# Routed experts in five widths, each visit's TensorE work in a branch of its own, rows beyond 256 in plain fp32

## The reference, cut to what matters

```python
logits = xf @ w_router + b_router                 # 2048 x 32
top_logit, top_e = lax.top_k(logits, TOP_K)       # 4 experts of 32 for each token
gates = jax.nn.softmax(top_logit, axis=-1)
# rows of x sorted by expert, group_sizes[e] rows for expert e
hu = lax.ragged_dot(xs, w_gate_up, group_sizes) + b_gate_up[e_sorted]   # 1024 -> 2048
gate = jnp.minimum(hu[:, :D_FF], 7.0)
up = jnp.clip(hu[:, D_FF:], -7.0, 7.0)
act = (up + 1.0) * gate * jax.nn.sigmoid(1.702 * gate)
y = lax.ragged_dot(act, w_down, group_sizes) + b_down[e_sorted]         # 1024 -> 1024
out = jnp.zeros_like(xf).at[tok].add(y * g_sorted[:, None])
```

## Time and profile before

| what | value |
|---|---|
| median of 3 runs | 5028.44 us |
| the profiled execution | 5037.48 us, span 5035.6 us |
| TensorE matmul busy | 4555.1 us, 90% of the span |
| VectorE / ScalarE / GpSimd busy | 3091.1 / 1819.6 / 877.7 us |
| mean granted TensorE clock | 0.942 of full speed |
| instruction fetch queue q8 | 69 packets, 1.13 MB |
| expert stage | from about 2135 to about 4885 us |

### The profile page before, as it was taken

One profiled execution on the slowest core, in us unless ns is written; L12 is line 12 of the kernel. 1 busy time (PEld: TensorE's weight loads), 2 busy tenths in 40 slices (PEclk: granted clock), 3 DMA queues, 4 the chain that ended last, 5 costly groups with the idle time before them and its releaser, 6 DMA issues. The chain is left out here.

```text
span 5035.6 us, 67493 instructions
## 1 busy us (share of the span) xinstructions
PE 4555.1 (90%) x23694; PEld 3404.2 (68%) x23695; DVE 3091.1 (61%) x4881; ACT 1819.6 (36%) x2636; POOL 877.7 (17%) x871
## 2 busy tenths in 40 slices
PE   8999877888888886479999999999999999999987
PEld 4444333334434443378999999999899999999971
DVE  3567545766667886356465655566576556665557
ACT  1222223333333332144343444344354434454330
POOL 0000012111111111222111211112122112121125
PEclk9999977898899888789999999999999999999996
DMA  5443111000000000165554554455556455664458
GB/s 177 136 121 117 53 58 28 14 18 23 14 16 14 17 19 9 25 225 176 183 175 165 210 198 160 158 200 175 180 197 217 167 180 186 215 217 175 142 187 345
DMA packets 524040, 666.04 MB, mean 132 GB/s; under 512 B 58176, under 2 KB 388416, under 8 KB 523872
## 3 DMA queue, kind: packets, MB, share of 16 engines
q1 hardware_dynamic: 400368, 484.87, 28.8%
q10 hardware_dynamic: 96960, 93.93, 5.7%
q0 software_dynamic: 26576, 85.56, 4.4%
HBM read 543.93 MB, written 120.36 MB: 132 GB/s over the span
## 5 line engine op out<-in xcount | busy, mean ns | idle before, releaser
L1766 PE MATMUL gu<-x_hi,w_hi 128*128 128x256 f32 (+2 forms) x4096 | 1230.9, 301 | 1.3 <-DVE x_lo L1848 1.3
L1767 PE MATMUL gu<-x_lo,w_hi 128*128 128x256 f32 (+2 forms) x4096 | 1231.2, 301 | 0.0
L1768 PE MATMUL gu<-x_hi,w_lo 128*128 128x256 f32 (+2 forms) x4096 | 1229.1, 300 | 0.0
L1843 DVE TENSOR_TENSOR w_lo<-w_raw,w_hi 128x2048 fp32r<-128x2048 f32 x386 | 874.6, 2287 | 530.4 <-ACT w_hi L1917 530.4
L1917 ACT ACTIVATE w_hi<-w_raw 128x2048 fp32r<-128x2048 f32 x386 | 726.8, 1907 | 280.0 <-PE gu L1768 198.7
L1766 PEld LDWEIGHTS gu<-x_hi,w_hi 128*128 128x128 f32 x4096 | 772.2, 189 | 2.5 <-issue 1.7
L1768 PEld LDWEIGHTS gu<-x_hi,w_lo 128*128 128x128 f32 x4096 | 772.7, 189 | 0.0
L1767 PEld LDWEIGHTS gu<-x_lo,w_hi 128*128 128x128 f32 x4096 | 770.4, 188 | 0.7
L1739 POOL TENSOR_TENSOR a_lo<-up,a_hi 128x384 fp32r<-128x384 f32 x256 | 396.8, 1550 | 1489.0 <-ACT a_hi L1929 1489.0
L1766 PE MATMUL yp<-w_hi,a_hi 128*128 128x512 f32 x1296 | 525.5, 405 | 0.0
L1767 PE MATMUL yp<-w_lo,a_hi 128*128 128x512 f32 x1296 | 514.5, 397 | 0.0
(11 more groups left out here) (283 smaller groups left out, 5409.4 us busy)
## 6 DMA issues: line engine op xcount, KB each, us to landing
w_raw<-w_gate_up SPq DMA_DIRECT2D x258, 1024.0 KB, 7.1
w_raw<-w_down SPq DMA_DIRECT2D x128, 1024.0 KB, 6.2
y_dram<-y_rows ACTq DMA_DIRECT2D x192, 256.0 KB, 2.7
y_dram<-zeros ACTq DMA_DIRECT2D x12, 2688.0 KB, 14.8
h_blk<-h_dram SPq DMA_DIRECT2D x32, 512.0 KB, 6.7
qi_dram<-qi_stage ACTq DMA_DIRECT2D x16, 640.0 KB, 3.2
x_in<-x SPq DMA_DIRECT2D x16, 512.0 KB, 6.6
w_in_sb<-w_in SPq DMA_DIRECT2D x4, 2048.0 KB, 14.1
```

What stands on the lines that cost most here:

```text
L1766: nc.tensor.matmul(out, s_hi_, m_hi, start=(n == 0), stop=False)
L1767: nc.tensor.matmul(out, s_hi_, m_lo, start=False, stop=False)
L1768: op = nc.tensor.matmul(out, s_lo_, m_hi, start=False, stop=(n == len(pairs) - 1))
L1843: nc.vector.tensor_tensor(w_lo[:, c % 2, cols], raw[:, c % 3, cols], w_hi[:, c % 2, cols].bitcast(F32), ALU.subtract).then_inc(s_lo, 1)
```

## The change

Five widths (256, 288, 320, 352, 384) take the place of three. The table gets two more comparisons for `kind` and a fourth column that says whether the visit has at most 320 rows. TensorE's whole visit (up part, transposes, down part) is put inside the branch of its width, so the text of a visit stands five times in the loop. For visits with 257 to 320 rows the two tiles at places 2 and 5 go: place 2 becomes `down_rest`, 16 plain fp32 matmuls of 64 weight columns (the rows beyond 256) by 512 moving columns of the raw down weights, one half of the outputs in partitions 0 to 63 and the other in 64 to 127; place 5 becomes the tiny matmul. The raw down weights must then stay until place 2 is done, which SP waits for. POOL copies the 64 columns for it, and ScalarE stores places 2 and 5 as two halves each, whose place in memory is chosen by the new column.

```diff
-WIDTHS = (2 * P, 2 * P + 64, ROWS)
+WIDTHS = (2 * P, 2 * P + 32, 2 * P + 64, 2 * P + 96, ROWS)
+REST = 64
...
                     if not first(v) or c >= 3:
                         sp.wait_ge(s_lo, 12 * v + 2 * (c - 3) + 2)
+                    if not first(v) and c in (1, 2):
+                        sp.wait_ge(s_g2, 6 * v - 3)
...
                         pool.wait_ge(s_ah, 8 * v + j + 1)
-                        nc.gpsimd.tensor_tensor(a_lo[:, j], up[:, j % 2], a_hi[:, j].bitcast(F32), ALU.subtract
-                                                ).then_inc(s_al, 1)
+                        nc.gpsimd.tensor_tensor(a_lo[:, j], up[:, j % 2], a_hi[:, j].bitcast(F32), ALU.subtract)
+                        nc.gpsimd.tensor_copy(a_rest[:, j], up[:, j % 2, 2 * P:2 * P + REST]).then_inc(s_al, 1)
...
+                def down_rest(v):
+                    pe.wait_ge(s_lo, 12 * v + 12)
+                    for k in range(KD):
+                        for h in range(2):
+                            w = raw[:, (4 + h) % 3].rearrange("p (k n) -> p k n", k=KD)
+                            op = nc.tensor.matmul(yp[h * REST:(h + 1) * REST, 0], a_rest[:, k], w[:, k],
+                                                  start=(k == 0), stop=(k == KD - 1))
+                    return op
...
-                    for n, width in enumerate(WIDTHS):
-                        with pe.If(kind == n):
-                            up(v, width)
+                def visit(v, width):
+                    up(v, width)
                     transpose_x(v + 1, 0)
                     transpose_x(v + 1, 1)
...
-                            if m < 2:
-                                down_tile(v, c, m).then_inc(s_g2, 1)
+                            if m < 2 or width > 2 * P + REST:
+                                op = down_tile(v, c, m)
+                            elif n == 2 and width > 2 * P:
+                                op = down_rest(v)
                             else:
-                                with pe.If(kind != 0):
-                                    down_tile(v, c, m).then_inc(s_g2, 1)
-                                with pe.Else():
-                                    nc.tensor.matmul(yp[:, n % 2, 0:EXPERTS], S["ident"][:], S["so_far"][:],
-                                                     start=True, stop=True).then_inc(s_g2, 1)
+                                op = nothing(n)
+                            op.then_inc(s_g2, 1)
...
+                def body(v):
+                    kind = look_up(pe, v, 2, len(WIDTHS) - 1)
+                    pe.wait_ge(s_xl, 8 * v + 8)
+                    for n, width in enumerate(WIDTHS):
+                        with pe.If(kind == n):
+                            visit(v, width)
...
                 def body(v):
+                    rest = look_up(act, v, 3, 1)
...
-                    nc.scalar.dma_start(
-                        D_["y"][bass.ds(v * ROWS + (n % 3) * P, P), (n // 3) * BANK:(n // 3 + 1) * BANK], y[:, slot]
-                    ).then_inc(s_yst[slot], 16)
+                    if n == 2:
+                        store_half(v, n, 0, 4, 0)
+                        store_half(v, n, 1, 5 - rest, rest)
+                    elif n == 5:
+                        store_half(v, n, 0, rest + 4, 1 - rest)
+                        store_half(v, n, 1, 5, 1)
+                    else:
+                        nc.scalar.dma_start(
+                            D_["y"][bass.ds(v * ROWS + (n % 3) * P, P), (n // 3) * BANK:(n // 3 + 1) * BANK], y[:, slot]
+                        ).then_inc(s_yst[slot], 16)
```

More of the change, by code:

```diff
@@ L1606, in _ @@
                 nc.vector.tensor_scalar(start[:], left[:], float(WIDTHS[0]), None, ALU.is_gt)
-                nc.vector.tensor_scalar(nth[:], left[:], float(WIDTHS[1]), None, ALU.is_gt)
+                nc.vector.tensor_scalar(S["meta"][:, :, 3], left[:], float(2 * P + REST), None, ALU.is_le)
                 dve.drain()
-                nc.vector.tensor_tensor(S["meta"][:, :, 2], start[:], nth[:], ALU.add)
+                for width in WIDTHS[1:-2]:
+                    nc.vector.scalar_tensor_tensor(start[:], left[:], float(width), start[:], ALU.is_gt, ALU.add)
+                    dve.drain()
+                nc.vector.scalar_tensor_tensor(S["meta"][:, :, 2], left[:], float(WIDTHS[-2]), start[:],
+                                               ALU.is_gt, ALU.add)
 def experts_stage(nc, A, S, D_):
@@ L1640, in experts_stage @@
         a_lo = sb("a_lo", [P, FF // P, ROWS], F32R)
+        a_rest = sb("a_rest", [P, FF // P, REST])
         y = sb("y_rows", [P, 2, BANK])
@@ L1802, in down_tile, with nothing @@
                                                  for k in range(KD)], 8 * v if n == 0 else None)
-                def body(v):
-                    kind = look_up(pe, v, 2, 2)
-                    pe.wait_ge(s_xl, 8 * v + 8)
-                    for n, width in enumerate(WIDTHS):
-                        with pe.If(kind == n):
-                            up(v, width)
+                def down_rest(v):
[6 more added lines that the diff above has]
+                    return op
+                def nothing(n):
+                    return nc.tensor.matmul(yp[:, n % 2, 0:EXPERTS], S["ident"][:], S["so_far"][:],
+                                            start=True, stop=True)
+                def visit(v, width):
+                    up(v, width)
                     transpose_x(v + 1, 0)
@@ L1929, in high_act, with store_half, store @@
                     nc.scalar.activation(a_hi[:, j], up[:, j % 2], ACT.Copy).then_inc(s_ah, 1)
-                def store(v, n):
+                halves = D_["y"].rearrange("(b r) (h n) -> b r h n", r=REST, h=2)
+                def store_half(v, n, lower, block, half):
+                    slot = n % 2
+                    block = 6 * v + block
+                    nc.scalar.dma_start(
+                        halves[slice(block, block + 1) if isinstance(block, int) else bass.ds(block, 1), :,
+                               slice(half, half + 1) if isinstance(half, int) else bass.ds(half, 1)
+                               ].rearrange("b r h n -> (b r) (h n)"),
+                        y[lower * REST:(lower + 1) * REST, slot]).then_inc(s_yst[slot], 16)
+                def store(v, n, rest):
                     slot = n % 2
@@ L1934, in store @@
                     if not first(v) or n >= 2:
-                        act.wait_ge(s_yst[slot], 48 * v + 16 * (n // 2))
+                        act.wait_ge(s_yst[slot], 64 * v + (0, 0, 16, 16, 48, 32)[n])
                     nc.scalar.activation(y[:, slot], yp[:, slot], ACT.Copy).then_inc(s_y, 1)
                     act.wait_ge(s_y, 6 * v + n + 1)
-                    nc.scalar.dma_start(
-                        D_["y"][bass.ds(v * ROWS + (n % 3) * P, P), (n // 3) * BANK:(n // 3 + 1) * BANK], y[:, slot]
-                    ).then_inc(s_yst[slot], 16)
+                    if n == 2:
[5 more added lines that the diff above has]
+                    else:
+                        nc.scalar.dma_start(
+                            D_["y"][bass.ds(v * ROWS + (n % 3) * P, P), (n // 3) * BANK:(n // 3 + 1) * BANK], y[:, slot]
+                        ).then_inc(s_yst[slot], 16)
                 def body(v):
+                    rest = look_up(act, v, 3, 1)
                     for c in range(4):
@@ L1959, in body @@
                     for n in range(6):
-                        store(v, n)
+                        store(v, n, rest)
                         if n in (0, 1, 3):
@@ L1973, in _ @@
                 n = over_visits(act, body)
-                act.wait_ge(s_yst[0], 48 * n)
-                act.wait_ge(s_yst[1], 48 * n)
+                act.wait_ge(s_yst[0], 64 * n)
+                act.wait_ge(s_yst[1], 64 * n)
                 nc.scalar.activation(y[:, 0, 0:1], y[:, 0, 0:1], ACT.Copy)
```

## The result

The changed kernel takes 5870.14 us, the median of 4 runs (5861.26 to 5880.06), beside 5026.77 for the kernel before on the same chip: 1.1677 times as long, 95% interval 1.1654 to 1.1699. Forecast was 5748, range 5440 to 6020. The profiled execution has a span of 5874.3 us.

What follows compares the result with a forecast made beforehand. TensorE's matmuls fill the expert stage and bound the span. Instruction misses adding 831 us, less 111 us saved by widths and down_rest, gave 720 us more: 5757 us profiled, 5748 us as median; range 5440 to 6020.

Steps and rivals of the forecast that it cites:

- The mechanism: TensorE's loop text grows from 1560 to 3600 instructions; skips between visits miss, 5 at each boundary; 831 us added.
- The capacity: TensorE's instruction store: no row shows more than 8 fetch packets held, against 14.1 packets of new loop text.
- The price of a miss: TensorE jump to absent code: 7.4 us during the held-back weight burst (1.5 misses), 5.1 us without traffic (3.5).
- the sum: Per boundary between visits: 29.0 us of misses, less 3.8 of lead, plus 1.9 of restart; net 27.1 us.
- The lead: TensorE's sequencer runs ahead of its queue at a boundary, hiding 3.8 us of the misses.
- Restart at half clock: TensorE's first work after a stop runs at half clock, 1.9 us extra on average.
- The end of the stage: After the last visit: 4 misses less 4 us of stores beside them, 16 us added.
- Widths: Up parts: 8 visits narrow from 320 to 288 (41 us saved), 3 from 384 to 352 (17 us).
- `down_rest`: Down part of 13 visits: 32 records, halves side by side, 6.9 us (in line 13.7); 53 us saved in all.
- Costed at nothing: SP's wait at cost 0; POOL's copy, ScalarE's column load and stores at 0, at most 1 us a visit.
- all resident: Rival: instruction store holds all 14 packets, skips cost 0.2 us each; 4927 us, faster; chance 0.13.
- Partly kept: Rival: instruction store keeps some packets, leaving 3.4 misses a boundary; 5471 us; chance 0.17.

Runs made afterwards that it cites:

- dead branches: Kernel before with one or two never-taken 256-row branches added to TensorE's loop: 5545.65 us (1.103) with one, 5688.54 us (1.1314) with two.
- shifted pair: Kernel before plus down_rest, three widths, old branch chain: 5498.69 us; the same with 12 tiny matmuls ahead of the loop: 4997.09 us (0.9942).
- nested chain: Changed kernel with its five Ifs nested as If and Else: 5205.66 us (1.0354); with a jump-back hint as well, 5145.40 us (1.0234).
- whole visits in three branches: Changed kernel with the old three widths instead of five: 5555.22 us, 1.1049.

## Why the prediction was right, point by point

- **The mechanism** was right. Text beyond what TensorE holds makes each long skip a fetch, (4 - k) + 1 + k' of them at a boundary; the branches show that count exactly, and the q8 forecast of some 400 packets became 460. The dead branches show the cause without any of the new work.
- **The capacity** was argued from "no row shows more than 8 held". The shifted pair shows 8 as the limit, and the cycles of 8, 10 and 11 of the other kernels agree. The Trainium skill, "Runtime: NRT & Kernel Launch", section "Instruction fetch mechanics", gives 2048 instructions in blocks of 16 KiB, which is 8 of these packets: the pair agrees. The same section of the Trainium skill has a taken branch stall when its target lies outside a window of two blocks; by that every loop of this size would stall, and the traces disagree: the shifted loop and that of the kernel before ran 30 turns without a fetch.
- **The price of a miss** was mis-sized: (1.5 x 7.4 + 3.5 x 5.1)/5 = 5.8 us forecast, 6.19 measured. Both prices were a little high (7.4 against 6.98 under traffic, 5.1 against 4.64 without). Their shares were wrong: I put 1.5 of 5 misses on the burst, and 85 of 153, 2.8 of 5, have the DMA engines at 0.8 or more. At a boundary the misses came to 31.0 us where the sum had 29.0.
- **A term left out:** the sum let a gap end with its last branch. Some 1.9 us a gap go by between the branches and behind the last one. The lead was right (3.8 forecast, 4.1 measured). The 31 gaps came to 893.7 us, 28.8 each, where the sum had 29.0 - 3.8 = 25.2. That is some 112 us, of the 122 between forecast and result: a little over half from the price of the misses, the rest from this term.
- **Restart at half clock:** 1.9 forecast; 1.5 measured at 288 rows, 2.0 at 256, 2.2 at 320 and 2.4 at 384.
- **The end of the stage:** 16 us forecast, 10.9 measured between the last visit and the next stage's first matmul.
- **Widths:** 51.4 us forecast for 288 rows, halfway; 51.1 measured in two visits of the nested chain that had no gap ahead. No 352-row visit without a gap was seen; 64.74, the mean of three, less a restart of 2.2 to 2.4 is 62.3 to 62.5, against 62.3 forecast.
- **`down_rest`:** 6.9 us forecast for 32 records, 7.09 measured; the other end, 13.7, falls. Two halves of 64 weight columns do run side by side.
- **Costed at nothing:** POOL's copy and SP's wait added no wait of TensorE, but SP's wait raised the misses' price by 60 us in all, an interaction the forecast saw only in part. ScalarE's stores and look-up are not free: 12 us, hidden here by the gaps and seen only when those were gone (0.4 us a visit, inside the forecast's bound of 1).
- **Rivals:** all resident (4927) needs some 3600 instructions held, and 8 packets are 2048. Partly kept (5471) didn't come in the changed kernel: every jump of the chain missed. Where the walk is shorter something of the kind is real: in the nested chain, and for some jumps of the whole visits in three branches.

## What to carry to other kernels

Count the instructions of the text that one turn of a loop walks over, skipped branches and the packet behind each jump included, and where the loop begins within a packet: up to the limit a jump took 0.07 to 0.22 us here, and one packet above it each turn paid 2.3 long branches of 5.4 us. A width, a tile shape or a specialisation that saves 4 us of work is worth less than one such miss. When a wait looks free, ask as well what its held-back transfers will meet.

## What was not expected of the hardware

- A never-executed branch costs 518 us of 5028, and a shift of the loop by 48 instructions is worth 502 us.
- A jump to code that isn't held takes 3.4 to 4.6 us on average with idle DMA engines and 6.3 to 7.6 with full ones. The 16 KB packets themselves took 0.9 to 2.5 us each in the changed kernel (median 1.4); what the rest of such a jump is, no trace here shows.
- The hint that a loop jumps back gained 60 us where the text didn't fit; without misses it wasn't tried.
- After stops of 11 to 45 us, in which the granted clock fell to 0.50, the restart costs 1.5 to 2.4 us, so the restarts together took back all that five widths had saved.
